# The even stage of a transformer kernel: the middle tap of a convolution is written by ScalarE out of PSUM, and the projection of the values moves between those of queries and keys

## The reference

```python
def even_mixer(x, w_in, gate_b, conv_w, rpb, w_out):
    a_qk, a_v, a_o, a_g, b_q, b_k, b_v = split_cols(
        x @ w_in, [2 * A_WIDTH, A_WIDTH, A_WIDTH, 4 * A_HEADS, B_WIDTH, B_WIDTH, B_WIDTH])
    a_qk = jax.nn.silu(centred_depthwise_conv(a_qk, conv_w))
    a_q, a_k = jnp.split(a_qk, 2, axis=-1)
    ...
    h2 = mlstm_chunkwise(both_dirs(q), both_dirs(k), both_dirs(v), log_i, log_f)
    ...
    a_out = jax.nn.sigmoid(a_o) * h
    b_out = neighbourhood_attention(b_q, b_k, b_v, rpb)
    return jnp.concatenate([a_out, b_out], axis=-1) @ w_out
```

## Time and profile before

| what | value |
|---|---|
| median of 3 runs | 3186.14 us (3183.77 to 3190.01) |
| the profiled execution, its own time | 3186.13 us |
| its span, first to last instruction | 3184.3 us |
| mean granted clock of TensorE | 0.972 of full |
| TensorE busy | 2990.0 us, 94% |
| VectorE busy | 905.5 us, 28% |
| ScalarE busy | 627.0 us, 20% |
| GpSimd busy | 1758.3 us, 55% |
| the projections of the even stage | from 20.1 to about 203.5 us of the span |

### The profile page before, as it was taken

How to read it: one execution, slowest core, us unless ns; L and a number is a source line. 1 busy time by engine, 2 the same in 40 slices (tenths; PEclk the granted TensorE clock), 3 DMA queues, 4 the chain that set the end, 5 groups by cost and what they waited for, 6 DMA issues and landing times.

```text
span 3184.3 us, 35491 instructions
## 1 busy us (share of the span) xinstructions
PE 2990.0 (94%) x14824; PEld 2482.5 (78%) x14824; DVE 905.5 (28%) x1463; ACT 627.0 (20%) x1311; POOL 1758.3 (55%) x1497
## 2 busy tenths in 40 slices
PE   7898999999999987899999999799999998899998
PEld 6776778888878656788888888678888886788887
DVE  3535402311023295123110021643110046530102
ACT  1224312210011162121110030341110032320100
POOL 5640383666665501835666656625666665456664
PEclk9999999999999998999999999899999998899999
DMA  4221241223223201413223233002223231022322
GB/s 145 67 80 40 67 146 53 93 96 103 93 93 101 80 1 49 150 45 101 93 93 106 85 108 93 27 14 93 93 93 106 86 107 66 27 93 93 99 100 79
DMA packets 182496, 267.11 MB, mean 84 GB/s; under 512 B 6592, under 2 KB 145984, under 8 KB 182336
## 3 DMA queue, kind: packets, MB, share of 16 engines
q1 hardware_dynamic: 174240, 243.28, 23.2%
q10 hardware_dynamic: 8096, 21.56, 2.0%
HBM read 262.73 MB, written 2.10 MB: 83 GB/s over the span
## 4 chain that ended last, share of the span: by engine, by line
PE 80%; DVE 13%; POOL 3%; issue 1%; ACT 1%; DMA 1%; DVEq 0%; ACTq 0%; POOLq 0%
PE PS L464 24%; PE PS L465 23%; PE PS L466 23%; PE PS L785 3%; POOL wlo L2143 2%; DVE PS L665 2%; DVE x_row L660 1%; PE PS L771 1%; DVE nmx L1435 1%; PE PS L1325 1%; DVE xT_lo L566 1%; PE PS L549 1%; DVE x_row L672 1%; PE PS L918 1%; POOL whi L2138 1%
## 5 line engine op out<-in xcount | busy, mean ns | idle before, releaser
L2138 POOL TENSOR_SCALAR whi<-raw 128x1024 fp32r<-128x1024 f32 x460 | 485.5, 1074 | 1318.5 <-DMA raw<-ffn_w 272.7
L2143 POOL TENSOR_TENSOR wlo<-raw,whi 128x512 fp32r<-128x512 f32 x920 | 1187.6, 1323 | 0.0
L464 PE MATMUL PS<-xT_hi,whi 128*128 128x512 f32 (+1 forms) x2304 | 856.7, 372 | 43.1 <-DVE xT_lo L566 30.7
L465 PE MATMUL PS<-xT_lo,whi 128*128 128x512 f32 (+1 forms) x2304 | 849.2, 369 | 0.0
L466 PE MATMUL PS<-xT_hi,wlo 128*128 128x512 f32 (+1 forms) x2304 | 849.0, 368 | 0.0
L464 PEld LDWEIGHTS PS<-xT_hi,whi 128*128 128x128 f32 x2304 | 442.3, 192 | 119.5 <-DVE xT_lo L566 33.9
L465 PEld LDWEIGHTS PS<-xT_lo,whi 128*128 128x128 f32 x2304 | 442.4, 192 | 71.2 <-issue 2.4
L466 PEld LDWEIGHTS PS<-xT_hi,wlo 128*128 128x128 f32 x2304 | 442.0, 192 | 70.5
L961 DVE TENSOR_TENSOR htmp<-sil,PS 128x512 f32<-128x512 f32 x88 | 56.5, 684 | 804.8 <-ACT sil L946 804.8
L464 PE MATMUL PS<-whi,xT_hi 128*128 128x512 f32 x672 | 264.4, 393 | 22.2 <-ACT a_pre L1026 16.3
L464 PE MATMUL PS<-whi,h_hi 128*128 128x512 f32 x704 | 274.1, 389 | 0.0
(11 more groups left out here) (359 smaller groups left out, 3124.7 us busy)
## 6 DMA issues: line engine op xcount, KB each, us to landing
raw<-ffn_w SPq DMA_DIRECT2D x66, 1024.0 KB, 5.0
raw<-ffn_w_gu SPq DMA_DIRECT2D x44, 1024.0 KB, 5.1
raw<-ffn_w_down SPq DMA_DIRECT2D x22, 1024.0 KB, 4.9
raw<-mem_wkv SPq DMA_DIRECT2D x16, 1024.0 KB, 5.2
raw<-even_w_in SPq DMA_DIRECT2D x14, 1024.0 KB, 5.2
raw<-ev_w_in SPq DMA_DIRECT2D x14, 1024.0 KB, 5.2
raw<-odd_w_in SPq DMA_DIRECT2D x12, 1024.0 KB, 5.2
raw<-od_w_in SPq DMA_DIRECT2D x10, 1024.0 KB, 5.1
```

Source lines behind the costliest of these rows:

```text
L464: pe.matmul(o, lhs[0], rhs[0], start=start, stop=False, skip_group_check=True)
L465: pe.matmul(o, lhs[0], rhs[1], start=False, stop=False, skip_group_check=True)
L2138: pool.tensor_scalar(whi[b][:, cs], raw[b][:, cs], 1.0, 1.0, ALU.mult, ALU.mult).then_inc(panel_hi, 1)
L2143: m = pool.tensor_tensor(wlo[b][:, cs], raw[b][:, cs], whi[b][:, cs].bitcast(F32), ALU.subtract)
```

## The change

Two edits. First, the list of jobs: what was one name `qk` becomes `q` and `k`, and the two panels of v are projected between the queries' two jobs and the keys' two jobs. Second, the convolution: VectorE's product of tap 0 goes. In its place ScalarE writes the middle tap, `w2` times the tile in PSUM, into `a_qk` just before it copies the tile into `a_pre`; VectorE then adds taps 0, 1, 3 and 4 to it.

```diff
-                jobs = t_jobs("T", W, 0, 1024, "act", "qk") + r_jobs("R", W, 1024, 512, "act", "v")
+                jobs = (t_jobs("T", W, 0, 512, "act", "q") + r_jobs("R", W, 1024, 512, "act", "v")
+                        + t_jobs("T", W, 512, 512, "act", "k"))
+                jobs[3].i, jobs[4].i = 4, 6
...
-                    if j.name == "qk":
+                    if j.name in "qk":
...
+                            act.activation(a_qk[:, i, :], PS[:, 2 * s + c, :], ACT.Copy, scale=pcol("conv_w", 16 + i, 1))
                             m = act.activation(a_pre[:, i % 2, 2:2 + S], PS[:, 2 * s + c, :], ACT.Copy)
...
+                conv_jobs = [j for j in jobs if j.name in "qk"]
                 for i in range(8):
...
-                        dve.wait_ge(evac_act, jobs[i // 2].done[1])
+                        dve.wait_ge(evac_act, conv_jobs[i // 2].done[1])
                     src, o = a_pre[:, i % 2, :], a_qk[:, i, :]
-                    step(dve.tensor_scalar(o, src[:, 0:S], pcol("conv_w", i, 1), None, ALU.mult))
-                    for k in range(1, 5):
+                    for k in (0, 1, 3, 4):
```

## The result

The changed kernel takes 3220.39 us in the median of 4 runs (3217.37 to 3222.8), the kernel before beside it 3186.32 us. The ratio is 1.0106, with a 95% interval from 1.0088 to 1.0123: slower by 34 us. The forecast was 3213, in a range from 3205 to 3221.

The account below looks back on a forecast made before the run. VectorE's convolutions were taken to bound the stretch. Waits before v (+4.3 us) and o (+20.6) and a second clock recovery (+2.4) sum to +27.3 on 3186.1 us: 3213 us, range 3205 to 3221.

Parts of the forecast that it names:

- The tap: Middle tap of the convolution: each copy's step gains 0.5 us on VectorE and loses 0.6 us on ScalarE, nearly cancelling.
- The first wait: Before v: TensorE stands 20.8 us until ScalarE has copied tile 3; v starts at 72.9, bk ends 4.3 us later.
- The second wait: Before o: TensorE stands 20.6 us until VectorE, behind convolutions and the gates' chain, has copied bk; o starts at 150.4.
- The clock's return: After each long wait, at v and o: the job takes 24.2 us instead of 21.8, 2.4 us for the clock's recovery.
- behind o nothing gives it back: Stages after o: they follow its end as before, so the full +27.3 us stays to the end.
- the shift at 175 us is not the shift at the end: Sign of a wrong forecast, after the end of o: a later stage absorbs or adds to the 27 us.
- The rule weighed: VectorE meeting GpSimd: the skill's "fully blocks" means the sum, 2.01 us per addition; the trace shows about 1.66.
- B: Where VectorE meets GpSimd, full turns: each addition takes 2.01 us instead of 1.66, +3.9 us, 3217.3 us; chance 0.07.
- E: Before o: wait longer than sized, convolutions and chain meeting GpSimd nearly throughout; 3219 to 3223 us; chance 0.10.
- A: The forecast itself: both long waits of TensorE, before v and before o, come as sized; 3213.4 us; chance 0.77.
- C: At the start of o: no wait, VectorE having copied bk by 129.8; only +4.3 us, 3190.4 us; chance 0.04.
- D: Faster: v starts by 62.2 after a 10 us wait, no wait before o; 3179.7 us; chance 0.02.

Follow-up runs that it names:

- second execution: The changed kernel run and profiled once more, unedited, beside the unedited kernel before on the same chip: 3217.86 us against 3181.24 us.

## Why the prediction was right, and where its sizes were off

**The bound.** Right: VectorE's queue behind the evacuations sets when TensorE goes on, in both kernels.

**The tap.** Right within its size for the new order: without it v starts 0.4 us later and o 2.1. In the old order it gives more than the prediction's minus 0.5 plus 0.6: there four products of VectorE lie on the path to v, three of them lengthened to 1.28 or 1.48 us, against one tap, and v moved by 4.1 us in the experiment with the tap alone. Not seen was that the taps also delay tile 1's copy, which the fourth job awaits in the old order (1.0 us). ScalarE's tap takes 0.69 us, and the copy behind it starts 0.58 us after it, close to the 0.61 from the row of line 1044.

**The first wait.** Expected 20.8 us, measured 21.4; v started at 73.83 and not at 72.9. The missing 0.9 us lie ahead of the convolutions: the first of the gates' logs on VectorE took 1.85 us beside GpSimd, where the kernel before had 0.68, so VectorE convolves from 66.4 and not from 65.2. This belongs to the order and not to the tap or to chance: in all six executions with the new order that instruction took 1.62 to 1.86 us, in all six with the old order 0.68 to 0.94. In the latter it began 0.09 to 0.37 us ahead of GpSimd's first `wlo` of that panel, in the former between 0.05 us ahead and 0.19 us behind. Why a tenth of a microsecond shifts with the order is open.

**The second wait.** Expected 20.6 us, measured 22.3, at the place and for the reason named; both experiments that take the chain or the copy out of the queue end it. The mis-sized terms: the convolutions of tiles 6 and 7 took 10.46 us and not 9.3, and the chain 20.0 and not 19.4. In the second execution they were 9.4 and 20.1. GpSimd began its panels at 113.95, 124.92 and 135.98 us, where 113.3, 124.3 and 135.2 had been expected. The chain's sum hides two errors that cancel: its first direction took 12.7 us and not 10.9 (from 131.39 to 144.09), its second 7.3 and not 8.4. So the 11.15 us that the prediction took as the worst for a direction is no bound. The trace named no releaser for this wait, where the prediction had expected `b_kT` in the list; with bk on ScalarE it did name one.

**The clock's return.** Expected 2 x 2.4 us over 21.8; measured 2.3 and 2.1.

**The sum.** 27.3 expected, 29.4 at the end of o: 1.2 us more for the meetings with GpSimd at tiles 6 and 7, 0.6 for the chain, and 0.9 from the later start of the queries, of which smaller pieces give 0.6 back, the clock's two returns 0.4 of them. The step that failed in size is "behind o nothing gives it back", in its silent other half: that nothing adds to it. The stages behind o have the same work, but the scan and the odd stage ran at a lower mean clock and added some 4 to 5 us in the first execution. The prediction had named the sign of it: the shift at 175 us is not the shift at the end. The time landed 7 us above the forecast, 2 of them from the stretch that was summed and 5 from behind it, for which the range held no term. That it still lies inside the range, by 0.6 us, is in part luck: the upper end stood for GpSimd beside everything, which did not happen.

**The rule weighed.** If the two engines took full turns, an addition beside GpSimd would take 2.01 us. The 32 additions of the changed kernel took at most 1.666, and the most with four slots was 1.782. Other instructions lost more: the first of the gates' logs took 1.85 us where the shortest is 0.68, and the sum with one of GpSimd's 1.26 is 1.94; the running maximum of line 1150 took 2.08 us, and 1.21 with GpSimd held back, where the sum is 2.47. What the Trainium skill says in "SBUF — State Buffer", section "SBUF: two separate sides", that the one that comes second "fully blocks", comes near to what the log shows; as a price for every meeting of a row it is too high.

**The rivals B and E.** The measured 3220.4 us is nearer to B's 3217 than to A's 3213, and lies inside E's 3219 to 3223, but it came by neither mechanism. The additions do not show B's price. E wants the second wait itself to be 6 to 10 us longer than sized; it was 1.7 us longer, the second half of the chain's last direction ran at its undisturbed lengths, and the 5 us that bring the time into E's band were added behind o.

**The rivals C and D.** C's condition, VectorE done with bk when TensorE is, was made true by moving the chain; the kernel then came to 3192, close to C's 3190.4, with a shift of 8.2 us at the end of o where C has 4.3. D did not come up.

## What to carry to other kernels

When jobs take slots in turn and evacuations stand in fixed queues, a new order has to be read through three lists at once: which slots each job gets, who frees them, and what stands ahead of that evacuation in its engine's own queue. Here moving one job changed the former owner of o's slot from v, which ScalarE had long evacuated, to bk, whose copy on VectorE had 21 us of other work ahead of it when bk ended. The wait that the move was meant to shorten went from 16.3 to 2.1 us with one more slot and the tap. And when a wait of TensorE goes, the engines that had rested get in each other's way sooner: with four slots half of the additions took 1.475 us or more, and a new wait of 2.5 us came up. Of the 16.7 us expected there about 12 came out at the end by the ratios, and no more when that wait was taken away as well; where the rest goes is not shown.

## What the runs showed of the hardware

VectorE's chain of small instructions on 4 partitions takes 14.2 us alone and 20.0 beside GpSimd's cutting, an addition or subtraction of 512 floats at 0.68 us against 1.4 to 1.7. Executions of one kernel scatter by up to 19 us (3183.8 to 3202.8 for the one with the chain first) on one core. The profiles show one source of such differences: stretches with the same work at a mean granted clock of 0.94 or 0.85 differ by 3.5 us in 56. VectorE's first log of the gates took 0.68 to 0.94 us in the six executions where it began 0.09 us or more ahead of GpSimd's `wlo`, and 1.62 to 1.86 in the six where it began 0.05 us ahead or later.
